# A hybrid block kernel on one core: the second attention's weighing in split halves, transposed, with the division last

## The reference

```python
sc = jnp.einsum('bhqd,bhkd->bhqk', qi, kb)
sc = jnp.where(valid, sc * scale + bias[None], NEG)
p = jax.nn.softmax(sc, axis=-1).astype(vb.dtype)
return jnp.einsum('bhqk,bhkd->bhqd', p, vb)
```

## Time and profile before

| | |
|---|---|
| median of three runs | 1927.69 us (1926.8 to 1928.15) |
| the profiled execution | 1927.73 us, its span 1925.9 us |
| busy, of the span | TensorE 99%, VectorE 52%, ScalarE 34%, GpSimd 52% |
| TensorE's granted clock | 0.998 |

### The profile page before, as it was taken

How to read it: one execution, slowest core, us unless ns; L and a number is a source line. 1 busy time by engine, 2 the same in 40 slices (tenths; PEclk the granted TensorE clock), 3 DMA queues, 4 the chain that set the end, 5 groups by cost and what they waited for, 6 DMA issues and landing times.

```text
span 1925.9 us, 26977 instructions
## 1 busy us (share of the span) xinstructions
PE 1899.8 (99%) x9708; PEld 1602.1 (83%) x9708; DVE 1009.0 (52%) x1863; ACT 664.0 (34%) x1260; POOL 998.5 (52%) x851
## 2 busy tenths in 40 slices
PE   8999999999999999999999999999999999999998
PEld 6788888888888988888878887888888888888886
DVE  6535663686555554454654457554444444444455
ACT  5135554546544453454521233331111111111134
POOL 4442237622222212112368884477777767777784
PEclk9999999999999999999999999999999999999999
DMA  4311113331111111102212213121211111211113
GB/s 138 110 44 29 33 39 104 83 124 42 42 42 51 28 40 50 43 19 67 77 50 55 55 28 132 54 66 44 75 50 52 44 44 45 76 55 44 55 33 131
DMA packets 148379, 115.26 MB, mean 60 GB/s; under 512 B 11528, under 2 KB 140048, under 8 KB 148256
## 3 DMA queue, kind: packets, MB, share of 16 engines
q1 hardware_dynamic: 135456, 93.34, 16.3%
q10 hardware_dynamic: 12800, 20.28, 3.2%
HBM read 105.15 MB, written 11.59 MB: 61 GB/s over the span
## 4 chain that ended last, share of the span: by engine, by line
PE 93%; DVE 3%; issue 1%; POOL 1%; ACT 1%; DMA 1%; SPq 0%; POOLq 0%; DVEq 0%; ACTq 0%
PE ps L1189 7%; PE ps L1063 6%; PE ps L1064 6%; PE ps L1065 6%; PE ps L1523 5%; PE ps L1522 5%; PE ps L1524 5%; PE ps L1485 5%; PE ps L1483 5%; PE ps L1484 5%; PE ps L1178 4%; PE ps L1046 3%; PE ps L1047 3%; PE ps L1048 3%; PE ps L1111 2%; PE ps L1112 2%
## 5 line engine op out<-in xcount | busy, mean ns | idle before, releaser
L821 POOL TENSOR_TENSOR w_hi<-raw,ones 128x512 fp32r<-128x512 f32 x100 | 112.7, 1127 | 636.2 <-PE ps L1065 484.2
L2936 DVE TENSOR_TENSOR X<-ps,X 128x1024 f32<-128x1024 f32 x112 | 137.2, 1225 | 204.7 <-PE ps L1524 204.7
L2127 ACT ACTIVATE ps<-ps 128x512 f32<-128x512 f32 x64 | 37.3, 582 | 510.9 <-DVE ps L2913 510.8
L1063 PE MATMUL ps<-h_hi,w_hi 128*128 128x512 f32 x480 | 191.7, 399 | 0.0
L1064 PE MATMUL ps<-h_lo,w_hi 128*128 128x512 f32 x480 | 188.1, 392 | 0.0
L1065 PE MATMUL ps<-h_hi,w_lo 128*128 128x512 f32 x480 | 187.8, 391 | 0.0
L1522 PE MATMUL ps<-hid_hi,slot_hi 128*128 128x512 f32 x448 | 174.3, 389 | 0.0
L1523 PE MATMUL ps<-hid_lo,slot_hi 128*128 128x512 f32 x448 | 174.3, 389 | 0.0
L1524 PE MATMUL ps<-hid_hi,slot_lo 128*128 128x512 f32 x448 | 174.3, 389 | 0.0
L969 POOL TENSOR_TENSOR slot_hi<-up,ones 128x512 fp32r<-128x512 f32 x88 | 91.7, 1042 | 114.5 <-PE ps L1524 112.0
L1189 PEld LDWEIGHTS ps<-v_seq,probs_t 128*128 128x128 f32 x1056 | 137.1, 191 | 11.9 <-issue 1.8
(11 more groups left out here) (453 smaller groups left out, 4931.8 us busy)
## 6 DMA issues: line engine op xcount, KB each, us to landing
raw<-in_w_in SPq DMA_DIRECT2D x88, 256.0 KB, 2.8
down_raw<-in_w_down SPq DMA_DIRECT2D x72, 256.0 KB, 2.8
up<-in_w_up SPq DMA_DIRECT2D x32, 512.0 KB, 4.1
raw<-in_w_out SPq DMA_DIRECT2D x32, 256.0 KB, 2.7
gate_ring<-in_w_in SPq DMA_DIRECT2D x24, 256.0 KB, 3.3
x_in<-in_x SPq DMA_DIRECT2D x8, 512.0 KB, 8.0
raw_b<-in_w_out SPq DMA_DIRECT2D x16, 256.0 KB, 2.7
x_store<-X ACTq DMA_DIRECT2D x8, 512.0 KB, 2.6
```

The costliest lines, as they stand in the source:

```text
L1063: pe.matmul(o, w1, h_hi[:, k, c], start=k == 0, stop=False)
L2936: dve.tensor_tensor(X[:, q], pair(q % 2), X[:, q], ALU.add).then_inc(x_added, 1)
```

## The change

In rounds 0 to 7 the weighing changes its form. Values are kept as rounded part and rest beside one another (`v_st`), and so are the transposed probabilities (`probs_ring`, three slots where there were four). The values are now the held operand (128 columns: rounded 64, rest 64) and the probabilities move (256 columns: rounded 128, rest 128), so one product gives all four combinations; the result is transposed already, with the dimension on the partitions. ScalarE rounds the probabilities (`probs_hi`), VectorE makes the rest (`probs_lo`). Of the four quarters three are summed: ScalarE copies the one on the upper partitions (`copy_low`), VectorE adds (`add_low`, `add_high`). The division comes last: the reciprocals are spread to rows, transposed (`inverse`, `turn_inverse`, in place of `turn_heads`) and multiplied in (`finish`).

The order changes too. On TensorE `turn(n-1)` stands directly behind `scores(n)`, ahead of the fill; `weigh_split(n-2)` stays behind it. On ScalarE `probs_hi(n-1)` stands ahead of exponential n, and `copy_low(n-2)` behind `events(n)`. On VectorE the order is `mask(n)`, `probs_lo(n-1)`, `inverse`, `events(n)`, `add_low`, `finish`, `add_high`. Buffers move to make room (`x_top1` among them), a set of semaphores is shared with `x_loaded`, and SyncE waits for round 7 before it loads the first branch weights.

```diff
@@ -366,9 +366,12 @@
...
-    v_seq = [t_at("v_seq0", [P, NB, P], F32, 28), place("v_seq1", [P, NB, P], F32, X0 + 24 * KB)]
+    v_swa = t_at("v_swa", [P, NB, P], F32, 28)
+    v_st = [t_at("v_st0", [P, NB, 2, 2, HD], F32R, 64), place("v_st1", [P, NB, 2, 2, HD], F32R, X0 + 24 * KB)]
...
-    probs_t = t_at("probs_t", [P, 4, 4 * P], F32, 40)
+    probs_ring = [t_at(f"probs_ring{n}", [P, 4, 2, P], F32R, kib) for n, kib in enumerate((28, 40, 44))]
+    o_sum = t_at("o_sum", [P, 2, P], F32, 72)
+    inv_rows = t_at("inv_rows", [P, 2, P], F32, 73)
...
@@ -1127,6 +1134,11 @@
...
+            def turn_inverse(pair_no, qb):
+
+                pe.wait_ge(inverted, NB * (pair_no - PAIRS) + qb + 1)
+                pe.transpose(ps[:, 3, 2 * P:3 * P], inv_rows[:, qb % 2], ident[:]).then_inc(heads_turned, 1)
...
+                def weigh_split(n):
+                    qb, hh, groups, g = units[n]
+                    pe.wait_ge(o_scaled, 1 + u0 + max(n - 1, 0))
+                    if hh == 1:
+                        pe.wait_ge(heads_stored, 1 + pair_no * NB + qb)
+                    for gi, (kb, cnt) in enumerate(groups):
+                        pe.wait_ge(turned_copied, 1 + group0 + (g + gi + 1))
+                        for b in range(cnt):
+                            mm = pe.matmul(bank(2 + hh, 2 * P),
+                                           buf["v"][st][:, kb + b, hh].rearrange("p a d -> p (a d)"),
+                                           probs_ring[(g + gi) % 3][:, b].rearrange("p a n -> p (a n)"),
+                                           start=(gi == 0 and b == 0),
+                                           stop=(gi == len(groups) - 1 and b == cnt - 1))
+                        mm.then_inc(pv_done, 1)
...
                 for n in range(16 + 2):
                     if n < 16:
                         scores(n)
+                    if 2 <= n <= 16 and kind != SWA:
+                        turn(n - 1)
...
-                    if n >= 2:
+                    if n >= 2 and kind == SWA:
                         weigh(n - 2)
...
-                    if n == 0 and pair_no not in (0, PAIRS):
+                    if n == 0 and kind == SWA and pair_no:
                         turn_heads(pair_no - 1, NB - 1)
...
                     if n == 1 and g_v is not None:
                         pe.wait_ge(v_ready, v_no)
-                    if 1 <= n <= 16:
+                    if n == 1 or n <= 16 and kind == SWA and n:
                         turn(n - 1)
-                    if n >= 4 and n % 2 == 0:
+                    if n >= 2 and kind != SWA:
+                        weigh_split(n - 2)
+                        if n % 2:
+                            turn_inverse(pair_no, (n - 3) // 2)
+                    if n >= 4 and n % 2 == 0 and kind == SWA:
...
@@ -1696,10 +1727,36 @@
+            def round_v(n, v):
+                act.wait_ge(v_turned, n)
+                act.activation(v[:, :, :, 0].rearrange("p b h d -> p (b h) d"),
+                               pair(3).rearrange("p (b d) -> p b d", d=HD), ACT.Copy).then_inc(v_hi_made, 1)
+
             def attention(kind, pair_no, group0, st, events):
 
                 u0, buf = pair_no * 16, BUF[kind]
+
+                def probs_hi(n):
+                    _, _, groups, g = UNITS[kind][n]
+                    for gi, (_, cnt) in enumerate(groups):
+                        act.wait_ge(turned, 1 + group0 + (g + gi + 1))
+
+                        act.wait_ge(pv_done, 1 + group0 + max(g + gi - 2, 0))
+                        act.activation(probs_ring[(g + gi) % 3][:, 0:cnt, 0],
+                                       bank(6 + (g + gi) % 2, cnt * P).rearrange("p (b n) -> p b n", n=P),
+                                       ACT.Copy).then_inc(p_hi_made, 1)
+
+                def copy_low(n):
+                    qb, hh, groups, g = UNITS[kind][n]
+                    act.wait_ge(pv_done, 1 + group0 + (g + len(groups)))
+                    if hh == 1:
+                        act.wait_ge(heads_turned, 1 + pair_no * NB + (qb + 1))
+                    act.wait_ge(o_scaled, 1 + u0 + max(n - 1, 0))
+                    act.activation(o_seq[0:HD, n % 2], ps[HD:P, 2 + hh, 0:P], ACT.Copy).then_inc(low_copied, 1)
+
                 for n in range(16 + 3):
+                    if 2 <= n <= 16 and kind != SWA:
+                        probs_hi(n - 1)
                     if n < 16:
                         qb, hh, _, _ = UNITS[kind][n]
                         cols = keys_of(kind, qb)[1] * P
@@ -1713,7 +1770,12 @@
                     events(n)
-                    if 1 <= n <= 16:
+                    if kind != SWA:
+                        if n == 1:
+                            probs_hi(0)
+                        if 2 <= n <= 17:
+                            copy_low(n - 2)
+                    elif 1 <= n <= 16:
                         _, _, groups, g = UNITS[kind][n - 1]
                         for gi, (_, cnt) in enumerate(groups):
...
                 def events(n):
                     if n == 0:
-                        store_v(r + 2, v_seq[st])
+                        if r == 0:
+                            act.wait_ge(staged, 7)
+                        round_v(r + 2, v_st[st])
...
                 c = slice(qb * P, (qb + 1) * P)
-                if pair_no < PAIRS:
-                    o = O[:, 4 + pair_no, c]
-                    ins = dve.tensor_tensor(o, bank(3, P), o, ALU.mult)
-                else:
-
-                    ins = dve.tensor_copy(O[:, pair_no % (2 * PAIRS), c], bank(3, P))
-                ins.then_inc(heads_stored, 1)
...
+                def inverse(qb):
+                    d = 2 * (qb % 2)
+                    dve.wait_ge(probs_ready, u0 + 2 * qb + 2)
+                    mine.done(dve.reciprocal(inv_total[:], total[:, d:d + 2]))
+                    mine.wait()
+                    dve.tensor_copy(inv_rows[:, qb % 2].rearrange("p (h d) -> p h d", h=2),
+                                    inv_total[:].rearrange("p (h a) -> p h a", a=1).broadcast_to([P, 2, HD])
+                                    ).then_inc(inverted, 1)
+
+                def add_low(n):
+                    qb, hh, _, _ = units[n]
+                    dve.wait_ge(low_copied, u0 - 16 * PAIRS + n + 1)
+                    low = o_seq[0:HD, n % 2]
+                    mine.done(dve.tensor_tensor(low, ps[0:HD, 2 + hh, P:2 * P], low, ALU.add))
+
+                def probs_lo(n):
+                    _, _, groups, g = units[n]
+                    for gi, (_, cnt) in enumerate(groups):
+                        slot = probs_ring[(g + gi) % 3]
+                        dve.wait_ge(p_hi_made, group0 - GROUP0[CHK] + (g + gi + 1))
+                        dve.tensor_tensor(slot[:, 0:cnt, 1],
+                                          bank(6 + (g + gi) % 2, cnt * P).rearrange("p (b n) -> p b n", n=P),
+                                          f32(slot[:, 0:cnt, 0]), ALU.subtract).then_inc(turned_copied, 1)
+
+                def add_high(n):
+                    qb, hh, _, _ = units[n]
+                    mine.wait()
+                    if hh == 0:
+                        dve.wait_ge(heads_stored, 1 + pair_no * NB + max(qb - 1, 0))
+                    dve.tensor_tensor(o_sum[hh * HD:(hh + 1) * HD, qb % 2], ps[0:HD, 2 + hh, 0:P],
+                                      o_seq[0:HD, n % 2], ALU.add).then_inc(o_scaled, 1)
+
+                def finish(qb):
+
+                    dve.wait_ge(heads_turned, 1 + pair_no * NB + (qb + 1))
+                    dve.wait_ge(o_scaled, 1 + u0 + 2 * qb + 2)
+                    dve.tensor_tensor(O[:, pair_no % (2 * PAIRS), qb * P:(qb + 1) * P], ps[:, 3, 2 * P:3 * P],
+                                      o_sum[:, qb % 2], ALU.mult).then_inc(heads_stored, 1)
+
+                if kind != SWA:
+                    for n in range(16 + 2):
+                        if n < 16:
+                            mask(n)
+                        if 2 <= n <= 16:
+                            probs_lo(n - 1)
+                        if n >= 2 and n % 2 == 0:
+                            inverse((n - 2) // 2)
+                        events(n)
+                        if n == 1:
+                            probs_lo(0)
+                        if n >= 2:
+                            add_low(n - 2)
+                        if n >= 4 and n % 2 == 0:
+                            finish((n - 4) // 2)
+                        if n >= 2:
+                            add_high(n - 2)
+                    finish(NB - 1)
+                    return
+
...
-                    if n == 1 and pair_no not in (0, PAIRS):
+                    if n == 1 and pair_no:
                         store(pair_no - 1, NB - 1)
...
+            def rest_v(r):
+
+                v = v_st[r % 2]
+                dve.wait_ge(v_hi_made, r + 1)
+                dve.tensor_tensor(v[:, :, :, 1].rearrange("p b h d -> p (b h) d"),
+                                  pair(3).rearrange("p (b d) -> p b d", d=HD),
```

(35 more changed lines are left out.)

## The result

The changed kernel takes 1948.62 us (median of 4 runs, 1947.56 to 1953.9) against 1927.31 for the kernel before on the same chip: ratio 1.0116, 95% interval 1.0097 to 1.0134, +21.3 us where +10.5 was forecast. The profiled execution took 1947.56 us with a span of 1945.8 us, 19.9 more than the span before.

The account below looks back on a forecast made before the run. TensorE, never idle in the eight rounds, was taken as the bound. From 1927.7 us, -50.7 (weighing) + 31.4 (ring) + 4.3 (start costs) + 25.5 (soft term) = +10.5 gave 1938 us; range 1914 to 1964, likeliest case 1932 to 1950.

Parts of the forecast that it names:

- soft term: Staging and other steps in the hand-over loop, with restart costs, delay TensorE: +25.5 us, between 12 and 49.
- part 3: Added sums and copies make a ScalarE-VectorE loop each iteration, 2.45 us against TensorE's 2.8, so staging shows: within the +25.5.
- the other places: Hand-over loop beyond q in rounds 1 to 6: round 0, table loads, values, forget steps, scan, end, restarts; 17.5 us.
- Part 1: TensorE's weighing: one 256-column product per block at 0.115 us instead of 0.211, 528 blocks: -50.7 us.
- the rival of a product of 256 columns that is no cheaper: TensorE's weighing costs what it did, so its gain is nil: +61, 1989 us; chance 0.03.
- Part 2: ScalarE's `probs_hi` waits for a ring slot, delaying exponential and TensorE's transpositions T(10) to T(15): +31.4, start costs +4.3 us.
- q's walk through the loop: Staging of next pair's q at n = 4 to 6 delays TensorE 1.3 us a round, rounds 1 to 6: +8.
- The values, ready late at n = 1: Values ready only after rounding and rest, later than TensorE's cover: 1.35 us in round 0, 1.0 in round 7.
- VectorE does not overlap its instructions: Rival: loop 0.25 us longer, each staging step shows, k no longer absorbed; soft term 49, 1962 us; chance 0.13.
- More air: Rival: 64x128 sums and hand-over nearer 0.1 than 0.28 us, soft term some 5: 1918 us; chance 0.29.
- cancel: Rival: the weighing's gain and the waits cancel, soft term 11 to 19: 1928 us; chance 0.17.
- Signs: Expected traces: 528 weighing records, TensorE idle 55 to 65 us at transpositions, VectorE busy near 400, stage about 506 us.

Follow-up runs that it names:

- e8: Changed kernel with four ring slots in all rounds, q's and k's rounding and rest cut to 8 of 1024 columns in rounds 1 to 6: 1899.55 us.
- e7: Changed kernel with q's rounding and rest cut to 8 of 1024 columns in rounds 1 to 6, leaving out part of q: 1936.51 us.
- e10: Changed kernel with the forget gate's logarithm and output gate's sigmoid as plain copies, so no table loads inside the rounds: 1945.43 us.
- e11: As e8 (four slots, q and k staging cut), with `copy_low` ahead of the staging on ScalarE: 1896.01 us.
- e9: Changed kernel with k's rounding and rest cut to 8 of 1024 columns in rounds 1 to 6, leaving out part of k: 1946.19 us.
- e2: Changed kernel with `copy_low(n-2)` ahead of the staging steps on ScalarE instead of behind them: 1942.0 us.
- e3: Changed kernel with four slots for the transposed probabilities in the causal rounds 4 to 7 only: 1931.83 us.
- e5: Changed kernel with four slots for the transposed probabilities in all eight rounds: 1920.51 us.
- e1: Changed kernel with exponential n ahead of `probs_hi(n-1)` on ScalarE: 2049.72 us.
- e4: As e1 (exponential ahead of the rounding), with the transpositions back behind the weighing on TensorE: 2056.93 us.

## Why the forecast was half the size

The runs bear the mechanism out at each place that the forecast named; what failed is the size of one term, the soft term of part 3. Loss in all: +21.3 + 50.7 = 72.0 us, forecast 61.2. Of the 10.8 between them 4.1 are q's staging, 5.4 the other places of part 3, and 1.3 ring and k's staging together.

- **Part 1, the weighing: right.** 0.118 us a block, forecast 0.115; at 0.118 the saving is 49.1 instead of 50.7. Nearly the whole of it is seen in e8's rounds 4 to 6, 6.7 of 6.9 us. With it falls the rival of a product of 256 columns that is no cheaper, and the count of columns by which the Trainium skill (FP8 and Floating Point Precision, TensorE Precision Notes) would have given nothing.
- **Part 2, the ring: the mechanism right.** In a causal round 4.2 measured against 4.35 with restarts. In all 28.1 when it alone is undone, against 35.7: in the band rounds k's staging stands behind the same wait and then shows instead. With both gone it is 37.0 in all (e8 less q's 12.1), 5.1 to 5.2 in each of rounds 3 to 6.
- **Part 3, the soft term: the step that failed**, +25.5 where 72.0 less the 35.7 of the ring leaves 36.3, inside its bounds of 12 and 49. In it q's walk through the loop, n = 4 to 7, was priced at 8 and is 12.1 (e7): its links are the right ones, but most were taken 0.1 to 0.2 us too short, and a loop with 0.3 us to spare passes each tenth on. The other places were priced at 17.5 and are 22.9 together.
- **Inside the other places** rounds 0 to 2 were priced too low: 7.2 against 4.3, 5.8 against 3.0 (1.6 of it the clock's drop in e8), 3.8 against 1.9; round 7 and the end, at 5.5 against 6.3, were not. The values, ready late at n = 1, were priced well: that iteration is 1.2 us longer than before in round 0 and 0.9 in round 7, forecast 1.35 and 1.0. Of the 22.9 the table loads are 3.2 (e10) and the order of `copy_low` 3.5, 1.6 of it the clock (e11). How the remainder divides between q and k of round 0, the forget steps, the scan and the end was not separated and stays open.
- **VectorE does not overlap its instructions: half right.** In the queue without a gap the 64x128 sums, with `finish` between them, start 0.20 to 0.21 apart at 0.28 each. A sum that directly follows the one it needs starts 0.31 behind it (641.43, 641.74), as the rival had feared for dependent pairs. The Trainium skill (VectorE: DVE Perf Modes, The DRAIN you can't avoid) says that the next operation starts only once the pipe is empty, but adds that one that is not held starts earlier; the prediction took only the first half, so a pair 0.20 apart does not speak against that page. Behind `rest_q` (1.22) the next started only after 1.25. The rival's price for k "no longer absorbed" did not come: 2.4 us (e9).
- **More air, cancel:** the sums cost 282 and 279 ns, the upper end of what the prediction took; there was no more air.
- **Signs.** The stage takes 515.8 us (436 to 951.8), forecast 506. Idle time of TensorE at the transpositions was forecast at 55 to 65 us; the groups show 26.1 for the matmuls and 47.0 for their weight loads, and in the stage TensorE is busy for 476.7 of 515.8 us, idle for 39.1. That is less than the loss, since a matmul that starts behind a gap is drawn longer: five transpositions of about 0.11 have a record of 0.77 us at 660.75. Distances between starts, as in the table, don't have this fault. VectorE's busy time in the stage is 384 us, forecast 400.

## What to carry to other kernels

When work moves to engines with "time to spare", a busy share (here VectorE's 384 of 516 us, 74%) says nothing of the cost. Walk the loop of hand-overs, and add up each engine's whole queue between two of its instructions that others wait for. The prediction did so and found every place. But where a loop of 2.5 us has only 0.3 to spare, errors of 0.1 a link return as whole microseconds by the third iteration: take the links from the nearest rows, starts and not durations, and let the forecast's range hold their sum. A ring's size is set by who frees a slot last in the new order: one more slot was worth 28 us here, more than half of what the matmuls had saved. And here the stalls undone together gave back more than the sum of what each gave alone (49.1 against 42.6): undo them together before calling one harmless.

## Hardware: the clock after an idle stretch

In four of the nine profiles of e2, e3 and e5 to e11, TensorE's granted clock fell to its lower level, 1.2 of 2.4 GHz, for some 3.5 us between 430 and 970 us; before and after show none there. Windows of e9 (busy us of each engine with counts, then granted clock, DMA share, GB/s), round 1 around the two table loads:

```profile
521.00:523.00 2.00, 2.00 (x14) 1.78 (x14) 1.76 (x7) 1.97 (x4) 0.00 (x0) 1.00 0.02 7
523.00:525.00 2.00, 1.16 (x8) 0.88 (x6) 0.85 (x3) 1.93 (x5) 0.00 (x0) 1.00 0.00 0
525.00:527.00 2.00, 0.85 (x4) 0.64 (x4) 1.97 (x7) 1.99 (x3) 0.00 (x0) 1.00 0.02 4
527.00:529.00 2.00, 1.88 (x8) 1.69 (x9) 1.88 (x7) 0.94 (x3) 0.00 (x0) 0.60 0.00 0
529.00:530.70 1.70, 1.70 (x6) 1.31 (x5) 0.42 (x1) 0.00 (x0) 0.00 (x0) 0.50 0.04 10
```

TensorE had been busy for 1.16 and 0.85 of two stretches of 2 us, then ran dense again, now at half the clock: 512-column products started 0.43 us apart instead of 0.23, and the iteration took 1.6 us longer than in after. The windows of after in the same place are alike (1.27 and 0.85 of 2 us), with the clock at 1.00 throughout. So much the same idle time brought it in one execution and not in the other. It fell at this place in e3, e8 and e9, 1.6 us each time by the distance of the scores, and near 950 us, behind the last round, in e9 and e10, where no cost stands out from the scatter. It is part of the scatter of the changed kernels and 1.6 of e8's 22.9 us. In e1 and e4, in which TensorE stands most, the granted clock from 430 us to the end of the rounds is 0.98 and 0.95. By that share of 625 and 638 us at most some 12 and 32 us of their time is the clock, an estimate, and the 7 us between the two may be nothing else.
